# A recurrence in 64x64 blocks: zero blocks dropped, and the next chunk's grams, masks and transposes set between this chunk's squarings

## The reference

```
def step(S, inp):
    r_t, d_t, k_t, v_t, kk_t, akk_t = inp
    s_kk = einsum('bhvk,bhk->bhv', S, kk_t)
    S = S * d_t - s_kk x akk_t + v_t x k_t
    return S, einsum('bhvk,bhk->bhv', S, r_t)
```

## Time and profile before

| | us |
|---|---|
| median of 3 runs | 2557.55 |
| lowest, highest | 2556.79, 2563.01 |
| the profiled execution, its own time | 2562.57 |
| its span | 2560.7 |
| TensorE busy (share of the span) | 2165.8 (85%) |
| VectorE busy | 697.4 (27%) |
| ScalarE busy | 471.6 (18%) |

### The profile page before, as it was taken

One profiled execution on the slowest core, in us unless ns is written; L12 is line 12 of the kernel. 1 busy time (PEld: TensorE's weight loads), 2 busy tenths in 40 slices (PEclk: granted clock), 3 DMA queues, 4 the chain that ended last, 5 costly groups with the idle time before them and its releaser, 6 DMA issues.

```text
span 2560.7 us, 32077 instructions
## 1 busy us (share of the span) xinstructions
PE 2165.8 (85%) x13482; PEld 1145.8 (45%) x13482; DVE 697.4 (27%) x1424; ACT 471.6 (18%) x1067; POOL 204.2 (8%) x240
## 2 busy tenths in 40 slices
PE   6899888877999878878777699999999688778773
PEld 3345788873645433222222344785654423222221
DVE  6203677675103321100000420462012311000002
ACT  3211344441102100100000200551021010000001
POOL 1000111101000011111111000000000111111100
PEclk9999899998999889989999899799999799999997
DMA  4020000012223479999999221002324699999995
GB/s 133 33 76 23 10 3 3 3 44 69 104 99 122 175 304 400 405 405 406 410 405 397 87 96 66 34 10 74 132 68 164 235 401 406 409 406 408 402 405 215
DMA packets 113062, 514.96 MB, mean 201 GB/s; under 512 B 20736, under 2 KB 21896, under 8 KB 95536
## 3 DMA queue, kind: packets, MB, share of 16 engines
q1 hardware_dynamic: 101824, 496.34, 49.6%
q0 software_dynamic: 10880, 16.81, 2.0%
q10 hardware_dynamic: 240, 0.07, 0.0%
HBM read 503.73 MB, written 28.31 MB: 208 GB/s over the span
## 4 chain that ended last, share of the span: by engine, by line
PE 63%; DMA 21%; DVE 7%; SPq 4%; issue 3%; ACT 1%; DVEq 0%; POOL 0%; POOLq 0%; ACTq 0%
DMA big<-in_moe_w 18%; PE ps L1597 11%; PE ps L1610 11%; PE ps L2002 10%; PE ps L1716 6%; PE ps L1930 4%; SPq L473 4%; PE ps L2023 3%; PE ps L1656 2%; PE ps L1842 2%; PE ps L1834 1%; PE ps L1807 1%; PE ps L1895 1%; DMA y_rows<-big 1%; PE ps L1907 1%
## 5 line engine op out<-in xcount | busy, mean ns | idle before, releaser
L2002 PE MATMUL ps<-big 128*64 128x512 f32 x2048 | 477.1, 620 | 72.7 <-DMA big<-in_moe_w 71.0
L2002 PEld LDWEIGHTS ps<-big 128*64 128x64 f32 x2048 | 163.2, 142 | 337.4 <-issue 321.4
L1597 PE MATMUL ps<-big 128*128 128x512 f32 (+1 forms) x768 | 278.0, 524 | 6.6 <-issue 6.6
L2023 PE MATMUL ps<-big 128*64 128x512 f32 x1024 | 255.9, 646 | 31.2 <-ACT big L988 31.2
L1610 PE MATMUL ps<-big 128*128 128x512 f32 x640 | 275.5, 592 | 0.0
L1597 PEld LDWEIGHTS ps<-big 128*128 128x128 f32 x768 | 146.5, 191 | 136.1 <-issue 128.6
L1610 PEld LDWEIGHTS ps<-big 128*128 128x128 f32 x640 | 121.5, 190 | 151.3 <-issue 151.2
L1716 PE MATMUL ps<-big 64*64 64x64 f32 x5632 | 178.5, 219 | 7.3 <-DVE big L1176 5.4
L1716 PEld LDWEIGHTS ps<-big 64*64 64x64 f32 x5632 | 171.2, 135 | 14.9 <-issue 8.6
L1489 DVE SCALAR_TENSOR_TENSOR big<-big,ps 128x256 f32<-128x256 f32 x64 | 26.9, 421 | 531.8 <-ACT big L981 531.8
L2023 PEld LDWEIGHTS ps<-big 128*64 128x64 f32 x1024 | 73.5, 146 | 172.2 <-issue 133.8
(11 more groups left out here) (323 smaller groups left out, 2171.8 us busy)
## 6 DMA issues: line engine op xcount, KB each, us to landing
big<-in_moe_w SPq DMA_DIRECT2D x192, 2048.0 KB, 33.8
big<-in_mx_wkv SPq DMA_DIRECT2D x8, 2048.0 KB, 7.9
big<-in_rw_wrkv SPq DMA_DIRECT2D x6, 2048.0 KB, 8.1
big<-in_mb_wqkv SPq DMA_DIRECT2D x6, 2048.0 KB, 8.3
big<-in_mx_wq SPq DMA_DIRECT2D x4, 2048.0 KB, 7.9
big<-in_mx_wo SPq DMA_DIRECT2D x4, 2048.0 KB, 8.2
h_rows<-big SPq DMA_DIRECT2D x16, 512.0 KB, 12.3
big<-y_rows SPq DMA_DIRECT2D x8, 1024.0 KB, 8.4
```

The lines of the kernel that those rows point to most:

```text
L1597: ins = mm(d[:, 0:n], lhsT=w[:, k, (j % 4) * P:(j % 4 + 1) * P], rhs=rhs[:, k, 0:n], start=k == 0, stop=k == KT - 1)
L2002: ins = mm(ps[2 + b][half * BR:(half + 1) * BR, :], lhsT=hgT[b][:, k], rhs=w13[set_][:, :, k, half * 256:(half + 1) * 256], start=k == 0, ...
L2023: ins = mm(ps[5 + b][half * BR:(half + 1) * BR, :], lhsT=hT[b][:, c0:c0 + BR], rhs=w2[set_][:, f, half * HB:(half + 1) * HB], start=f == 0 ...
```

## The change

- *Blocks.* beta, kappa, X, Y, Tm, N, K, Bn, bt and kt are stored as 64x64 blocks, one for each head, without the zero blocks: a group's matrix is 128x256 instead of 128x512. alpha and rho are read from `ar` itself; their copies go. The masks shrink to 128x64, and the clearing of the four block matrices goes.
- *Matmuls.* Everything on TensorE is `each_head`. The grams are 64x64 weights with 128 columns, one matmul for each head. The transposes become matmuls with the identity as the moving operand (`turned` for beta and kappa, `y0` for X).
- *Order.* Units of chunk c+1 stand between the levels of chunk c: gram_b after level 0, gram_k after level 1, turned after level 2, y0 after level 3. On VectorE the masks stand after levels 0 and 1, and `prepare` of chunk c+2 between t6 and the update of S. On ScalarE the copies of `turned` and the exponentials of chunk c+2 stand between x3 and x4, and y0's copy after x4. All these units use bank 0 of their group.
- *Copies.* `ar` and `dec` have three buffers, X, Y, Tm, N, K, Bn, bt and kt two.
- *Loops.* ScalarE and VectorE code is unrolled over the chunks. In o and s the terms with u come last. GpSimd waits for `beta` instead of `kappa1`.

```diff
+    prep = ("a_rest", "a_first", "rho", "beta", "kappa")
+    pe += of(0, "gram_b", "gram_k", "turned", "y0")
+    act += of(0, "decay", "growth") + of(1, "decay", "growth") + of(0, "bt", "kt", "y0")
+    dve += of(0, *prep, "x0", "t0", "bn", "n", "k") + of(1, *prep)
+    for c in range(CH):
+        ahead = lambda *steps: of(c + 1, *steps)
+        pe += of(c, "x1", "y1") + ahead("gram_b") + of(c, "x2", "y2", "t2") + ahead("gram_k")
+        pe += of(c, "x3", "y3", "t3") + ahead("turned") + of(c, "x4", "y4", "t4") + ahead("y0")
+        pe += of(c, "y5", "t5", "t6", "rhs", "u", "o", "s")
+        act += of(c, "x1", "x2", "x3") + ahead("bt", "kt") + of(c + 2, "decay", "growth") + of(c, "x4") + ahead("y0")
+        act += of(c, "y5", "rhs", "u", "o")
+        dve += of(c, "y1") + ahead("x0", "t0", "bn") + of(c, "y2", "t2") + ahead("n", "k")
+        dve += of(c, "y3", "t3", "y4", "t4", "t5", "t6") + of(c + 2, *prep) + of(c, "s_add", "s")
...
-            for m in (b["alpha"], b["rho"], b["beta"], b["kappa"]):
-                eng.memset(m.rearrange("p q h t -> p (q h t)"), 0.0)
             eng.memset(b["S"].rearrange("p q t -> p (q t)"), 0.0).then_inc(pre_done, 1)
...
+            def exponentials(g, c):
+                b = groups[g]
+                if c == 0:
+                    act.wait_ge(dve_done[g], 1)
+                else:
+                    wait_dve(act, g, c - 1, "kappa")
+                lam = chunk_of(lam_all, g, c)
+                A(b["dec"][c % 3], lam, ACT.Exp).then_inc(act_done[g], 1)
+                A(b["gro"], lam, ACT.Exp, scale=-1.0).then_inc(act_done[g], 1)
...
+            def prepare(g, c):
+                b = groups[g]
+                ar, dec = b["ar"][c % 3], b["dec"][c % 3]
+                kk, ak, kc, rc = (chunk_of(r, g, c) for r in (kk_all, ak_all, k_all, r_all))
+                wait_act(dve, g, c, "decay")
+                V.tensor_tensor(ar[:, :, 0, 1:], kk[:, :, 1:], dec[:, :, :-1], ALU.mult).then_inc(dve_done[g], 1)
+                V.tensor_copy(ar[:, :, 0, 0:1], kk[:, :, 0:1]).then_inc(dve_done[g], 1)
+                V.tensor_tensor(ar[:, :, 1, :], rc, dec, ALU.mult).then_inc(dve_done[g], 1)
+                wait_act(dve, g, c, "growth")
+                if c:
+                    wait_pe(dve, g, c - 1, "turned")
+                V.tensor_tensor(b["beta"], ak, b["gro"], ALU.mult).then_inc(dve_done[g], 1)
+                V.tensor_tensor(b["kappa"], kc, b["gro"], ALU.mult).then_inc(dve_done[g], 1)
...
             def each_head(dst, width, *terms):
 
                 for q in range(GP):
                     for i, (lhs, rhs) in enumerate(terms):
                         for h in range(2):
-                            r, c0 = slice(h * L, (h + 1) * L), q * width + (h * L if rhs.ndim == 4 else 0)
-                            moving = rhs[r, q, h, :] if rhs.ndim == 4 else rhs[r, q]
-                            ins = mm(dst[r, c0:c0 + L], lhsT=lhs[r, q, h, :], rhs=moving, start=i == 0,
+                            r = slice(h * L, (h + 1) * L)
+                            ins = mm(dst[r, q * width:(q + 1) * width], lhsT=lhs[r, q], rhs=rhs(r, q), start=i == 0,
                                      stop=i == len(terms) - 1)
                 return ins
...
+            turn = lambda r, q: ident[r, r]
+
+            def gram_b(g, c):
+                b = groups[g]
+                wait_dve(pe, g, c, "beta")
+                if c:
+                    wait_act(pe, g, c - 1, "y0")
+                each_head(ps[4 * g], P, (b["beta"], of(b["ar"][c % 3]))).then_inc(pe_done[g], 1)
+
+            def gram_k(g, c):
+                b = groups[g]
+                wait_dve(pe, g, c, "kappa")
+                wait_dve(pe, g, c, "bn")
+                each_head(ps[4 * g], P, (b["kappa"], of(b["ar"][c % 3]))).then_inc(pe_done[g], 1)
+
+            def turned(g, c):
+                b = groups[g]
+                wait_dve(pe, g, c, "k")
+                each_head(ps[4 * g][:, 0:GP * L], L, (b["beta"], turn))
+                each_head(ps[4 * g][:, GP * L:2 * GP * L], L, (b["kappa"], turn)).then_inc(pe_done[g], 1)
+
+            def y0(g, c):
+                wait_act(pe, g, c, "kt")
+                each_head(ps[4 * g], L, (groups[g]["X"][c % 2], turn)).then_inc(pe_done[g], 1)
...
+            ahead = (gram_b, gram_k, turned, y0)
+            for unit in ahead:
+                for g in range(2):
+                    unit(g, 0)
             for c in range(CH):
...
                 for i in range(6):
                     for g in range(2):
...
+                        level(g, c, i)
+                    if i < 4 and c + 1 < CH:
+                        for g in range(2):
+                            ahead[i](g, c + 1)
```

More of the change, by code:

```diff
@@ L112, in chunk_steps @@
 def chunk_steps():
[L114 to L126, removed]
+    pe, act, dve = [], [], []
+    of = lambda c, *steps: [(step, c) for step in steps if c < CH]
+    prep = ("a_rest", "a_first", "rho", "beta", "kappa")
[11 more added lines that the diff above has]
+        dve += of(c, "y3", "t3", "y4", "t4", "t5", "t6") + of(c + 2, *prep) + of(c, "s_add", "s")
+    return [{step: i + 2 for i, step in enumerate(steps)} for steps in (pe, act, dve)]
 def trunk(nc, x_in, mem, positions, ln_mix, ln_mem, ln_memkv, ln_ffn, rw_mu, rw_w0, rw_w1, rw_w2, rw_a0, rw_a1,
@@ L286, in trunk @@
             views, end = {}, 0
[L287 to L298, removed]
+            home = region(1 if g == 0 else 4, 2)
+            for name, copies in ([("ar", 3), ("dec", 3)]
+                                 + [(m, 2) for m in ("X", "Y", "Tm", "N", "K", "Bn", "bt", "kt")]
+                                 + [(m, 1) for m in ("beta", "kappa", "gro", "rhs", "u", "S")]):
+                size = GP * L * (2 if name == "ar" else 1)
+                made = []
+                for _ in range(copies):
+                    r = home[:, end:end + size]
+                    end += size
+                    made.append(r.rearrange("p (q s t) -> p q s t", q=GP, s=2) if name == "ar"
+                                else r.rearrange("p (q t) -> p q t", q=GP))
+                views[name] = made if copies > 1 else made[0]
+            assert end <= 8192
             groups.append(views)
@@ L610, in _ @@
             link(triangle(before[:], ones[:], ALU.is_gt, 0.0, mult=-1, pattern=[[1, P]]))
[L611 to L615, removed]
+            for m, full in ((m_strict, before), (eye, ident)):
+                for h in range(2):
+                    r = slice(h * L, (h + 1) * L)
+                    link(pool.tensor_copy(m[r, :], full[r, r]))
+            link(pool.tensor_tensor(m_incl[:], m_strict[:], eye[:], ALU.add))
             link(pool.tensor_scalar(m_minus[:, 0], m_strict[:], -1.0, None, ALU.mult))
@@ L1168, in _ @@
+            for g in range(2):
+                prepare(g, 0)
+            for g in range(2):
+                masked_b(g, 0)
+            for g in range(2):
+                masked_k(g, 0)
+            for g in range(2):
+                prepare(g, 1)
+            for c in range(CH):
                 for i in range(6):
                     for g in range(2):
[L1170 to L1173 removed]
@@ L1174, in _ @@
-                        if i:
-                            wait_pe(dve, g, c, f"t{i + 1}")
-                            V.tensor_tensor(b["Tm"], bs(g, 3), b["Tm"], ALU.add).then_inc(dve_done[g], 1)
+                        level(g, c, i)
+                    if i < 2 and c + 1 < CH:
+                        for g in range(2):
+                            (masked_b, masked_k)[i](g, c + 1)
+                if c + 2 < CH:
+                    for g in range(2):
+                        prepare(g, c + 2)
```

236 lines of the change are left out of this document (106 added, 130 removed).

## The result

The changed kernel takes 2491.64 us (median of 4 runs, 2484.91 to 2496.52) against 2557.17 us (4 runs, 2554.19 to 2563.01). The ratio is 0.9739, its 95% interval 0.9711 to 0.9768. The forecast was 2498 us. The profiled execution took 2484.91 us, with a span of 2483.2.

The account below looks back on a forecast made before the run. Chunk preparation and the loop through VectorE held TensorE back in the recurrence. 7 x (36.07 - 28.1) = 55.8, + 1.6 + 1.9 = 59.3 us gain, giving 2498 us; 8-in-10 range 2484 to 2526.

Parts of the forecast that it names:

- The bound: Recurrence: chunks of 36.07 us, 13 us of it preparation; after the change TensorE's 27.1 us of work sets the pace.
- The pace: TensorE in the recurrence: one 64x64 record issued every 29.3 ns, so a chunk's 704 records take 20.6 us.
- The grams: Grams as 64 half-tile records of 128 columns per chunk: 57 ns each, 3.65 us, the two heads overlapping.
- rival 1: The two heads' gram matmuls do not overlap: 3.5 us more a chunk, 28 us in all, 2526 us; chance 0.08.
- The period: One chunk of the recurrence: 27.1 us of TensorE work + 0.34 + 0.3 + 0.3 = 28.1 us.
- the handing over: Switching between the thirteen units of a chunk on TensorE: 0.3 us a chunk, range 0 to 1 us.
- The places that wait: Within a chunk: gaps stay at level 5 (0.34 us) and u (0.3 us); level 4 is tightest, 0.7 us of slack.
- The ends: Outside the steady loop: clearing gone gains 1.9 us, last chunk gains 1.6, preparation of chunk 0 gains nothing.
- Gaps (2): Ahead work on ScalarE and VectorE keeps TensorE's 2.55 us of gaps a chunk: 2511 us; chance 0.10.
- Columns for nothing (3): New 128-column gram pairs cost no more than 64-column ones: 14 us more gain, 2484 us; chance 0.04.
- A transfer (4): After the recurrence, the gain is given back to a transfer that was hidden: 2557 us; chance 0.02.
- The clock (5): Clock falls under half-tile work alone in the recurrence: 26 us more a chunk, up to 2706 us; chance 0.04.

Follow-up runs that it names:

- serial: Changed kernel with small blocks kept but all units of a chunk at its own start, nothing ahead: 2527.41 us, ratio 0.9883.
- prep_ahead: Changed kernel with only the next chunk's exponentials and scaling ahead; grams, masks and transposes follow the update of S: 2501.19 us, ratio 0.9782.
- heads_apart: Changed kernel with the four gram matmuls of one head before those of the other, instead of in turn: 2497.25 us, ratio 0.9762.
- heads_far_apart: Changed kernel with the eight gram matmuls of head 0 of both groups before the eight of head 1: 2515.97 us, ratio 0.9844.

## Why the prediction was right

- *The bound.* Said: TensorE's issue takes the place of the preparation and of the loop through VectorE. It has 97.9% of the chain over one chunk. serial and prep_ahead show that both parts were needed.
- *The pace.* 29.3 ns a record was taken; `turned` shows (358.58 - 356.72) / 64 = 29.1.
- *The grams.* 57 ns taken, 55 measured; two records start every 109 ns, where 112 to 116 was said. The heads of a pair overlap (rival 1 is refuted), though they write one PSUM bank; heads_apart and heads_far_apart show that the price comes from overlap. The Trainium skill, TensorEngine Tiling (Array Packing), section Restrictions and Gotchas, would have different row tiles never in one bank at a time. The measurement decides: these two tiles lie in different row halves and in different column halves, and they run together in one bank. Tiles that share a column half were not run.
- *The period.* 28.1 taken, 27.42 measured: 800 records at 29.2 ns and 64 at 55 make 26.9, and 0.6 are gaps. Of the 0.7 too much, 0.3 is the handing over, of which the trace shows nothing, and 0.15 the grams; the rest is the other records, the two gaps and rounding (the terms as written add up to 28.0).
- *The places that wait.* Level 5 and u, as said; levels 2 and 4 don't wait. (Level 1 of the next chunk does not read S, as the prediction has it: S is first read by rhs, and what level 1 would miss is VectorE's copy of Y, queued behind S.) VectorE's 16.7 and ScalarE's 10.0 us a chunk were 16.2 and 9.3.
- *The ends.* The clearing gave its 1.9, the last chunk 1.3 and not 1.6. The preparation of chunk 0, for which no gain was taken, came within 0.4 us of before, in part by luck: 1.5 us gained up to the first gram, 1.9 lost behind it. One VectorE step of 1.46 us beside GpSimd is 1.0 of that; the prediction had seen such a step in before (0.99) and looked for it in the loop only. There it falls on the multiply of S (L1218, 1.3 us once in each of six chunks), and no wait of TensorE follows.
- *The sum.* 59.3 predicted; 60.55 + 1.5 + 1.3 = 63.35 in the trace and 65.5 between the medians. The period gave 4.8 more than predicted, the ends 0.7 less. The last 2 us lie outside the recurrence or in the spread of executions.
- *The rivals.* Gaps (2): 0.6 a chunk, not 2.55. Columns for nothing (3): 128 columns cost 53 ns, 64 cost 29. A transfer (4): the shift of 62 us is kept through the first expert stage. The clock (5): 1.00 through 213.9 us of half-tile work alone.

## What to carry to other kernels

When a loop-carried chain holds work that does not depend on what is carried, measure the chunk against TensorE's bare issue time (records times the pace read off a full stretch): the difference, here 36.07 against 26.9 us, is what reordering can give, and smaller copies alone reach only part of it. Put the independent units where a level would wait, and ask of each what it covered before it is moved again: y0 moved into one gap opened another. And issue matmuls of opposite quarters of the array in turn, since the same 32 records cost 1.75, 2.25 or 3.01 us by order alone.

## What the hardware showed beyond that

- Matmuls in different quarters need not start in the program's order: a record for the free quarter started three records early, with 8 and with 16 records of the other quarter in a row, and no earlier. Hence 55, 70 and 94 ns a record with 1, 4 and 8 matmuls of a head in a row, at some 110 ns within a quarter. In heads_far_apart 29 records took 2.95 us at granted clock 1.00 (from 301.64) and 5.62 at 0.50 (from 289.28).
- A VectorE step over 128x256 between two SBUF operands took 1.46 to 1.49 us when it began just behind the start of a GpSimd instruction, and 0.42 elsewhere; a copy of four columns took 1.03 in place of 0.17. Every slowed step of 128x256 ended 0.28 us behind the GpSimd instruction, whether it took 0.81 or 1.49; steps that read PSUM kept 0.42.
- The same instructions between the first and the second expert stage differed by 12 us between two executions, by how long the granted clock stayed low in it and around it (6.8 and 27.3 us in the attention; 3.4 was the shortest). A difference of under 10 us between two profiled spans of this kernel says nothing until that stretch has been looked at.
